# Four matmuls of 256 columns with an unread result, added to each step of the differential attention

## What is computed

```python
def diff_attention(xn, positions, w_qkv, q_norm, k_norm, lq1, lk1, lq2, lk2, subln, w_o, lambda_init):
    ...
    def block(args):
        q_blk, bi = args
        s = jnp.einsum('bqhcd,bkhcd->bhcqk', q_blk, k, preferred_element_type=F32) * scale
        ...
        s = jnp.where(kpos[None, :] <= qpos[:, None], s, -jnp.inf)
        p = jax.nn.softmax(s, axis=-1)
        attn = p[:, :, 0] - lam * p[:, :, 1]
        return jnp.einsum('bhqk,bkhe->bqhe', attn, v)
    ...
    o = rms_norm(o, subln) * (1.0 - lambda_init)
    return o.reshape(B, T, DIFF_HEADS * DIFF_V_DIM).astype(xn.dtype) @ w_o
```

## Time and profile before

| | us |
|---|---|
| runs of the kernel before | 2348.61, 2346.84, 2339.27 |
| median | 2346.84 |
| span of the profiled execution, first to last instruction | 2340.4 |
| the differential attention in it | about 708.8 to 765.3 |

### The profile page before, as it was taken

One profiled execution on the slowest core, in us unless ns is written; L12 is line 12 of the kernel. 1 busy time (PEld: TensorE's weight loads), 2 busy tenths in 40 slices (PEclk: granted clock), 3 DMA queues, 4 the chain that ended last, 5 costly groups with the idle time before them and its releaser, 6 DMA issues. The chain is left out here.

```text
span 2340.4 us, 26194 instructions
## 1 busy us (share of the span) xinstructions
PE 1999.2 (85%) x9196; PEld 1644.2 (70%) x9196; DVE 1613.6 (69%) x1547; ACT 1224.6 (52%) x1310; POOL 91.2 (4%) x71
## 2 busy tenths in 40 slices
PE   5658977998758659999999999999998979778868
PEld 5648866777645548787787878788787867566657
DVE  4677357887466468787887868788787875545444
ACT  3421213444434247576776757677676754463364
POOL 1000000000020000000000000000000000210030
PEclk9868668999885779999999999999999999768967
DMA  5400017876440079799897979899797944113320
GB/s 191 144 0 1 28 33 260 287 279 211 128 142 1 1 265 381 280 355 352 295 378 270 376 261 375 303 343 372 274 373 280 376 168 157 59 36 109 124 72 19
DMA packets 239046, 488.93 MB, mean 209 GB/s; under 512 B 7585, under 2 KB 12706, under 8 KB 238848
## 3 DMA queue, kind: packets, MB, share of 16 engines
q1 hardware_dynamic: 231216, 458.21, 55.0%
q0 software_dynamic: 7760, 29.80, 3.5%
HBM read 485.36 MB, written 2.62 MB: 209 GB/s over the span
## 5 line engine op out<-in xcount | busy, mean ns | idle before, releaser
L1902 DVE TENSOR_TENSOR expert_weights_low<-BIG,expert_weights_high 128x2048 fp32r<-128x2048 f32 x336 | 768.6, 2291 | 133.2 <-ACT expert_weights_high L2273 132.5
L2273 ACT ACTIVATE expert_weights_high<-BIG 128x2048 fp32r<-128x2048 f32 x336 | 642.4, 1918 | 248.3 <-PE bank L968 240.8
L966 PE MATMUL bank<-expert_weights_high,expert_x_high 128*128 128x512 f32 x896 | 357.0, 398 | 18.3 <-DVE expert_x_low L1910 18.3
L967 PE MATMUL bank<-expert_weights_high,expert_x_low 128*128 128x512 f32 x896 | 350.4, 391 | 0.0
L968 PE MATMUL bank<-expert_weights_low,expert_x_high 128*128 128x512 f32 x896 | 350.3, 391 | 0.0
L1429 DVE TENSOR_TENSOR weights_low<-BIG,weights_high 128x2048 fp32r<-128x2048 f32 (+2 forms) x100 | 219.4, 2194 | 177.2 <-ACT weights_high L2064 176.0
L2064 ACT ACTIVATE weights_high<-BIG 128x2048 fp32r<-128x2048 f32 (+2 forms) x100 | 183.5, 1835 | 293.6 <-PE bank L968 210.4
L966 PE MATMUL bank<-weights_high,x_high 128*128 128x512 f32 (+2 forms) x608 | 243.3, 400 | 35.9 <-DVE weights_low L1429 14.2
L967 PE MATMUL bank<-weights_high,x_low 128*128 128x512 f32 (+2 forms) x608 | 239.5, 394 | 0.0
L968 PE MATMUL bank<-weights_low,x_high 128*128 128x512 f32 (+2 forms) x608 | 239.4, 394 | 0.0
L966 PEld LDWEIGHTS bank<-expert_weights_high,expert_x_high 128*128 128x128 f32 x896 | 168.9, 189 | 56.2 <-issue 20.2
(11 more groups left out here) (378 smaller groups left out, 2569.9 us busy)
## 6 DMA issues: line engine op xcount, KB each, us to landing
BIG<-in_o_moe_gate SPq DMA_DIRECT2D x112, 1024.0 KB, 5.2
BIG<-in_o_moe_up SPq DMA_DIRECT2D x112, 1024.0 KB, 5.2
BIG<-in_o_moe_down SPq DMA_DIRECT2D x112, 1024.0 KB, 5.4
BIG<-in_w_ada POOLq DMA_DIRECT2D x12, 2048.0 KB, 9.1
BIG<-in_w_in SPq DMA_DIRECT2D x20, 1024.0 KB, 5.0
BIG<-in_o_w_qkv SPq DMA_DIRECT2D x12, 1024.0 KB, 5.1
BIG<-in_e_w_in SPq DMA_DIRECT2D x10, 1024.0 KB, 5.0
BIG<-in_e_ffn_gate SPq DMA_DIRECT2D x10, 1024.0 KB, 5.0
```

The source lines that it names most:

```text
L966: mm(b, high_l, high_r, start=start, stop=False, skip_group_check=not check)
L967: mm(b, low_l, high_r, start=False, stop=False, skip_group_check=not check)
L1902: tt_(WL[q % E_SPLITS], half(q % E_SLOTS), WH[q % E_SPLITS].bitcast(F32), SUB)\
L2273: f(WH[q % E_SPLITS], e_tile(act, it, E_TILES[q]), ACT.Copy).then_inc(w_high, 1)
```

## The change

Ahead of the wait for the weights of step i, and behind the wait for the bank that the transposes go to, TensorE computes four products of `x_high`'s first tile: 128 rows, 128 output rows, 256 columns, in fp32r. They are written to the bank's second half, columns 256 to 511, which the step's one or two transposes (columns 0 to 255) don't use and nobody reads. This is done where `n_c` is 1, so in the 16 steps of the differential attention.

```diff
@@ -1017,6 +1017,8 @@
                 def transposes(i):
                     g, m = steps[i]
                     b = fill(pe, (tag, "weightsT", i))
+                    for _ in range(4 if n_c == 1 else 0):
+                        mm(b[:, T:2 * T], XTH[:, 0, 0:P], XTH[:, 0, :], start=True, stop=True)
                     pe.wait_ge(ready, base + i + 1)
                     for c in range(n_c):
                         for k in range(m + 1):
```

## The result

| | before | with the four matmuls |
|---|---|---|
| median, us (5 runs each) | 2341.17 | 2355.56 |
| lowest to highest, us | 2339.19 to 2348.61 | 2352.14 to 2359.24 |
| ratio to before | | 1.0051 [1.0031, 1.0072] |
| profiled execution, span, us | 2340.4 | 2350.3 |
| attention stage, first L1009 to the squaring | 708.87 to 765.27: 56.40 | 710.65 to 775.89: 65.24 |

What follows compares the result with a forecast made beforehand. TensorE, nearly full at 1.2 GHz, was taken to bound the attention stage's loop. Six pairs of steps at 1.48 us (8.9) plus 0.4 at the end give +9.3 on 2346.84, so 2356.1 us; range 2340 to 2362.

Steps and rivals of the forecast that it cites:

- the term for the ends of the stage: Attention stage, steps 0, 13, 14 and 15: the first three free in idle time, the last about 0.4 us.
- Clock: Attention stage: TensorE's granted clock stays at 0.50 (1.2 GHz) from 714 to about 774 us.
- the rival: Attention stage: added work raises TensorE to 2.4 GHz, VectorE bounds at 5.2 us a head, time 2341 us; chance 28%.
- The two rows that spoke against it: Next layer's attention, 2290 to 2297, full yet at 0.50; small matmuls, 250 to 325, also at 0.50.
- Price of one: Added matmuls in a step: 0.85 us for four, plus 0.1 for the first load, 0.95 behind scores.
- the rival built on unhidden loads: Added matmuls: each weight load waits for the matmul ahead, four cost 1.28 us, time 2362.5 us; chance 6%.
- A head: Attention loop: second step adds 0.95 us, first 0.53 after 0.42 of cover; 1.48 longer, 6.70 to 8.2 us.
- as the sign said: VectorE in a head: its idle before L1490 would be longer by about 1.5 us.
- gone except at steps 0 and 14: TensorE's transposes: the wait of L1025 for L1517 would vanish in all but these two steps.
- The sum: Attention stage: six pairs at 1.48, 8.9 us, plus 0.4 at the end, +9.3 us; nothing behind swallows it.
- From span to median: Whole kernel: median 2346.84 lies 6.4 us above the profiled span 2340.4, so +9.3 gives 2356.1 us.
- Faster, same, slower: Whole kernel: chance 0.07 faster by over 0.5%, 0.73 within 0.5% (11.7 us), 0.20 slower by over 0.5%.

Runs made afterwards that it cites:

- e3_two: Two matmuls in each step instead of the change's four; 2345.79 us, ratio to before 1.0013.
- e7_second_steps: The change's four matmuls only in steps 1, 3, 5, 7, 9 and 11; 2345.19 us, ratio to before 1.0002.
- e6_ends: The change's four matmuls only in steps 0, 13, 14 and 15; 2345.21 us, ratio to before 1.0001.
- e5_four_again: The kernel of the change, unchanged, measured a second time; 2349.84 us against 2344.87 before, ratio 1.0022.
- e13_four_third: The kernel of the change, unchanged, measured a third time; 2351.99 us against 2343.95 before, ratio 1.0037.
- the first comparison: The change against the kernel before, 5 runs each; 2355.56 us against 2341.17, ratio 1.0051.
- the three ratios: The unchanged kernel of the change, compared with before three times; ratios 1.0051, 1.0022 and 1.0037.
- e2_first24: The change with 24 matmuls in step 0 and four in each other step; 2328.97 us, ratio to before 0.9952.
- e12_first24_again: The kernel with 24 matmuls in step 0 and four in each other step, measured again; 2330.32 us, ratio to before 0.9940.
- e11_first24_two: The change with 24 matmuls in step 0 and two in each other step; 2344.37 us, ratio to before 0.9995.
- e9_to_projection: e2_first24 plus 72 matmuls ahead of the output projection's wait for the normalised result; 2333.03 us, ratio to before 0.9942.

## Why the prediction was right

It forecast 2356.1 us, no measurable change more likely than slower, and a mechanism: TensorE's queue grows at 1.2 GHz. The mechanism and its main terms stood; the absolute number came out as near as it did partly by luck, and so did the term for the ends of the stage.

- **Clock.** 0.50 through all the heads, as forecast: from 715.2 to 773.2 us. The rise at 773.2, before the stage's end, was not forecast. The chance of 28% for the rival was not idle, since six a step raise the clock. The two rows that spoke against it pointed the right way.
- **Price of one.** Forecast 0.213 us apart plus 0.1 for the first load, 0.95 a step. The answer on line L1021 in 727 to 729 us of the changed kernel gives the durations in ns, least, median and greatest:

```profile
L1021 PE MATMUL bank<-x_high x4: 415/415/580, 727.5 to 728.3; 128*128 128x256 f32 x4
```

  The first is 165 ns longer than the others, and the group takes 1.02 us: 0.165 + 4 x 0.214. But the 0.1 stood for a full load in place of the transposes' shorter one, and the transposes' records have become shorter behind the group, 0.63 for 0.69 us and 0.41 for 0.45. So the 0.95 is to be held against the 0.96 by which the second step grew: the term stood. The loads run beside the matmuls: in the same answer the four loads, of 0.29 to 0.33 us each, start between 727.5 and 728.1 us, the last of them 0.2 us ahead of its own matmul and so while the one ahead is in the array; and the matmuls start 0.21 us apart. The rule that was weighed (the Trainium skill, "TensorE: Matmul & The Clock Gate", "Packing small matmuls — row/col tiling": overlap only between different row groups) does not hold in this run, and the rival built on unhidden loads falls. What lengthens the first record stays open. The prediction put it to the change from 64-row scores, but in step 14, where the group follows the values of 128 rows, the first record is nearly as long (770.2 to 771.6 us):

```profile
L1021 PE MATMUL bank<-x_high x4: 415/415/561, 770.3 to 771.1; 128*128 128x256 f32 x4
```

- **A head.** Forecast 0.95 + 0.53 = 1.48, 6.70 to 8.2; measured 0.96 + 0.56 = 1.52, 8.22. e3_two (0.67 for 0.64) and e7_second_steps (0.56 for 0.53) give the same working at other sizes. VectorE's idle before its two L1490 grew by 1.56 us a head (2.03 + 0.86 for 1.33), as the sign said. One reading was loose: the 2.84 us of VectorE were taken to 727.27, the start of the transpose's load, while its L1515 ends at 727.15; nothing else hangs on it.
- **The ends.** Forecast: steps 0, 13 and 14 free, 0.4 us for step 15. The size was about right and the place was wrong. From the start of the last 256-column L1015 to step 15's transposes it was 5.77 us before (756.63 to 762.40); with the change it is 6.28 (767.47 to 773.75), and in e6_ends 6.29 (761.17 to 767.46): 0.5 us are paid. From there to the squaring it is 2.14 us in both, for 2.87 before, since the clock had risen to 1.00: that gives 0.7 us back, which is why e6_ends looks free. The rows point to step 13. Its four hold up ScalarE's copy of its transposes, 2.88 us behind that L1015 (770.35) where before it is 1.93:

```profile
758.56 0.38 ACT L2100 ACTIVATE BIG<-bank 128x256 f32<-128x256 f32 x1 [1.70 <-issue]
```

  Step 15's exponentials stand behind this copy on ScalarE, and start 3.62 us behind the same L1015 for 3.01. No run had the four in one of these steps alone, so this is a reading and not a test. The sign "gone except at steps 0 and 14" held: the load of step 14's transpose still waits 0.31 us.
- **The sum.** Forecast +9.3 for the stage; measured +8.8, 8.9 and 8.8. The pairs gave 6 x 1.52 = 9.1, the ends +0.5, and the clock's rise at 773.2, ahead of the last values, took 0.7 back (before it stayed at 0.50 until 782.1). That rise was in no term of the sum; that the total is near hangs on its being worth no more than this.
- **From span to median.** This step failed, without harm. I put the median 6.4 us above the span; but a run's time is 1.8 us above its own span (2352.14 against 2350.3), and 2346.84 was a high middle of three runs. Later medians of before are 2341.17 to 2344.87. From 2340.4 + 1.8 the sum would have been 2351.5, which is near e5_four_again and e13_four_third and 4 below the first comparison.
- **Faster, same, slower.** Of the three ratios two lie within 0.5% of no change and the first 0.01% beyond it, so by the prediction's own bound of 0.5% "no measurable change" was the right call, near its edge. With 10 to 12 runs a difference under that bound can be told: all three intervals exclude no change.
- **The rival's price.** The clock's rise was put at 5.2 us a head with VectorE as the bound, 10.5 us off the stage if it is there from the first head; e2_first24 shows 5.17 and 10.4. The 5.17 is the working, the 10.4 in part luck: the six heads gave 8.5 and not 9 (two of them took 5.63 and 5.41), the start 0.7 and the end 1.2. What I lacked was that staying up and coming up are two questions. The advice for the clock (the Trainium skill, "TensorE: Matmul & The Clock Gate", "Why this matters for your kernels": keep TensorE busy without pause) is borne out as far as the direction goes, by e2_first24; the row of 57.20 busy us of 61 at 0.52 shows again that busy time in the profile does not tell.

## What to carry to other kernels

Work that nobody reads is paid in full, less the loop's one wait, as long as the clock stays and it stands in the queue of the engine on the path: here 1.52 us a head at 1.2 GHz, though TensorE seemed to wait. At 2.4 GHz VectorE was the bound, and the same work lay in TensorE's spare time. Before filling holes for the clock, look at the clock in the stage itself, and try the hole in which it falls (the wait at the start) together with the filling behind it, since each alone gave nothing here; then vary the amount, for the sign can turn. And judge a local change by its stage in the trace, which repeated to 0.1 us, rather than by three runs that scatter by 10.

## What the runs showed that I had not expected

- Four matmuls a step hold the clock at 1.00 when it is up (e2_first24, e12_first24_again) and do not bring it up when it is down (58 us at 0.50 with the change, through all its heads; at the stage's end it rose). Two did not hold it in the one trace (e11_first24_two: up at 720.1, down at 727.0).
- More added work is cheaper: the stage takes 65.2 us with four a step, 49.3 with six, 50.9 with eight. A head at 2.4 GHz is 5.15 us with six, near the 5.17 at which VectorE bounds, and 5.63 with eight, where VectorE waits for the scores again (0.5 us before every second L1490). Whether six beats eight as a kernel is not shown: the trace with six is that of its fastest run, and the ratios, 0.9974 and 0.9969, can't be told apart.
- A higher clock in a stage that other engines read out is worth little: in e9_to_projection 1.7 us off the transposes came out as 0.42 us.
- The same program differs by 9 us behind a stage that repeats to 0.1 us (1565.1 to 1574.4). Its clock fell and rose there at other times: behind the stage it was back at 1.00 at 793.7, 787.7 and 793.2 us in the three executions of the change. That is not all of it, since the first and the last of these are 4.5 us apart behind the stage. The mean granted clock of the whole execution goes with its length: 0.883, 0.892 and 0.886 for spans of 2350.3, 2341.2 and 2345.0 us, and among the twelve runs of e5_four_again from 0.892 for 2342.98 us to 0.882 for 2355.11. So the scatter goes with how much of the kernel runs at 1.00; in which other stages was not looked up.
